# Two transformer blocks on one core: the expert stage's DMAs change queues, its last three blocks stay on chip, and a selection is computed earlier

## The reference, cut to what matters

```python
def moe(x2, w_router, router_bias, w1, w3, w2):
    expert_idx, gate_w = route(x2, w_router, router_bias)      # 2 of 16 experts for each token
    ...
    # the 1024 assignments are sorted by expert and padded to whole blocks
    def run_block(args):
        e, toks = args
        xb = x_pad[toks]
        h = jax.nn.silu(xb @ w1[e]) * (xb @ w3[e])
        return h @ w2[e]
    yb = lax.map(run_block, (blk_e, slot_tok.reshape(n_blk, MOE_BLOCK)))
    y = yb.reshape(-1, D) * slot_gate[:, None]
    return jnp.zeros((N + 1, D), x2.dtype).at[slot_tok].add(y)[:N]
...
        x = layer_norm(DN_ALPHA * x + mix, ln1_g[l], ln1_b[l])
        ffn = moe(x.reshape(B * S, D), w_router, router_bias, w1[l], w3[l], w2[l]).reshape(B, S, D)
        x = layer_norm(DN_ALPHA * x + ffn, ln2_g[l], ln2_b[l])
```

## Time and profile before

| | us |
|---|---|
| median of 3 runs (3739.15 to 3741.57) | 3740.26 |
| profiled execution, its own time | 3743.44 |
| its span in the trace | 3741.4 |
| mean granted TensorE clock over the span | 0.942 |

### The profile page before, as it was taken

How to read it: one execution, slowest core, us unless ns; L and a number is a source line. 1 busy time by engine, 2 the same in 40 slices (tenths; PEclk the granted TensorE clock), 3 DMA queues, 4 the chain that set the end, 5 groups by cost and what they waited for, 6 DMA issues and landing times. The chain is left out here.

```text
span 3741.4 us, 67546 instructions
## 1 busy us (share of the span) xinstructions
PE 3362.5 (90%) x25782; PEld 1878.2 (50%) x25783; DVE 1370.1 (37%) x2629; ACT 906.5 (24%) x1563; POOL 288.8 (8%) x289
## 2 busy tenths in 40 slices
PE   8998999787879989997877699999998788999998
PEld 5445444566754454445666434434444577444443
DVE  1564112545533751113544531011457555410002
ACT  1124111455521161113544410000113422100000
POOL 1000001322130000003322110000000000000000
PEclk9999999799989999997999889999999878999999
DMA  7112222698431103232987222245111000122221
GB/s 262 57 45 80 71 75 112 241 381 348 186 143 68 56 12 124 78 135 113 379 334 315 86 69 72 74 93 149 68 68 55 1 0 1 56 70 76 78 79 67
DMA packets 79881, 446.92 MB, mean 119 GB/s; under 512 B 10416, under 2 KB 22328, under 8 KB 32896
## 3 DMA queue, kind: packets, MB, share of 16 engines
q0 software_dynamic: 37024, 242.40, 16.9%
q1 hardware_dynamic: 39792, 199.77, 15.1%
q10 hardware_dynamic: 2928, 3.07, 0.2%
HBM read 412.05 MB, written 33.16 MB: 119 GB/s over the span
## 5 line engine op out<-in xcount | busy, mean ns | idle before, releaser
L902 PE MATMUL pb<-arena,streamed 128*128 128x512 f32 x1408 | 612.2, 597 | 7.4 <-DVE arena L1858 6.6
L902 PEld LDWEIGHTS pb<-arena,streamed 128*128 128x128 f32 x1408 | 268.6, 191 | 350.3 <-issue 337.7
L801 PE MATMUL pb<-arena,xT 128*32 x3008 | 357.5, 278 | 56.8 <-issue 33.2
L556 PE MATMUL pb<-xT,streamed 128*128 128x512 f32 x832 | 369.5, 603 | 0.0
L801 PE MATMUL pb<-streamed,xT 128*32 128x128 f32 x9024 | 360.1, 278 | 5.5 <-issue 5.5
L801 PEld LDWEIGHTS pb<-arena,xT 128*32 128x32 f32 x3008 | 325.9, 112 | 75.9 <-issue 69.3
L727 PE MATMUL pb<-xT,streamed 128*128 128x512 f32 x768 | 337.1, 597 | 2.5 <-ACT arena L1237 2.5
L801 PEld LDWEIGHTS pb<-streamed,xT 128*32 128x32 f32 x9024 | 329.2, 112 | 4.8 <-issue 4.8
L928 PE MATMUL pb<-arena,streamed 128*128 128x512 f32 x704 | 306.5, 598 | 8.3 <-DMA streamed<-in_w_tail 5.8
L1257 ACT ACTIVATE streamed<-arena 128x3072 f32 x94 | 260.1, 2767 | 57.5 <-issue 48.9
L556 PEld LDWEIGHTS pb<-xT,streamed 128*128 128x128 f32 x832 | 160.1, 194 | 202.8 <-issue 202.7
(11 more groups left out here) (357 smaller groups left out, 3617.7 us busy)
## 6 DMA issues: line engine op xcount, KB each, us to landing
arena<-in_w_moe POOLq DMA_DIRECT2D x192, 1024.0 KB, 10.6
streamed<-in_w_tail SPq DMA_DIRECT2D x87, 1024.0 KB, 4.9
streamed<-in_w_layer SPq DMA_DIRECT2D x78, 1024.0 KB, 4.9
xT<-xs_dram SPq DMA_DIRECT2D x22, 512.0 KB, 11.7
ys_dram<-xT SPq DMA_DIRECT2D x82, 128.0 KB
xs_dram<-lnw POOLq DMA_DIRECT2D x12, 512.0 KB, 17.6
lnw<-in_ln_par POOLq DMA_DIRECT2D x4, 1024.0 KB, 5.9
rel_dram<-arena POOLq DMA_DIRECT2D x1, 4092.0 KB, 88.0
```

The lines of the kernel that those rows point to most:

```text
L556: last = mm(pb[bank][:, 0:cols], unit(w, u, k), rhs[:, k * cols:(k + 1) * cols], start=(k == 0), stop=(k == KC - 1))
L801: last = mm(pb[m][r0:r0 + MOE_BLOCK, 0:FW], rows, w, start=(k == 0), stop=(k == KC - 1))
L902: last = mm(pb[3 * u + s][:], unit(w, u, k), xn[:, k * S:(k + 1) * S], start=(k == 0), stop=(k == KC - 1))
```

## The change

- The expert weights (`load`, `arrived`) move from GpSimd's program to SyncE's, between two halves of the layer weights' `stream`. Row loads and stores (`load_rows`, `store_y`) move from SyncE to GpSimd. The patterns and sizes of all these DMAs stay.
- Blocks 44 to 46 (ON_CHIP = 3) stay in SBUF in `y_last`, 96 rows of 1024. ACT writes each with four copies of 32x256 in place of one of 128x256. 44 blocks are stored, not 46. `last_sel` picks 96 rows. `last_tile` takes 96 rows and 2 matmuls of 512 columns for each tile, where it took 32 rows and 4 of 256. Of the gathers GpSimd now waits for the 44 stores, and for the last block of expert 14, whose weight slot they overwrite.
- DVE computes `sel` before the block tables. PE waits for `route_ready` behind its row selection. ACT runs one tiny Silu right behind the first w1 relay.
- At the end DVE handles one tile after the other: gathered rows, sums, statistics, norm. PE alternates `last_tile` and the transposes.

```diff
@@ constants and buffers
+ON_CHIP = 3
+STORED = N_BLK - ON_CHIP
+OUT_OF = [(STORED + 3 - s) // 4 for s in range(4)]
+LAST = STORED * MOE_BLOCK
...
+        y_last = am[:, 3 * FW:3 * FW + D]
...
@@ sync: what it issues in a layer
-                stream(1, 12)
-
-                def load_rows(j):
...
+                def load(e, p):
+
+                    sp.dma_start(piece(e, p), a["w_moe"][bass.ds((l * N_EXP + e) * PIECES + p, 1)]
+                                 .rearrange("a p n -> p (a n)")).then_inc(expert_loaded[p // 2], 16)
+
+                def arrived(e, m):
+
+                    sp.wait_ge(expert_loaded[m], (l * N_EXP + e + 1) * 32)
                     alone(sp)
-                    sp.dma_start(xs, xs_dram[j * P:(j + 1) * P, :]).then_inc(xs_loaded, 16)
...
+                    sp.sem_inc(expert_here[m], 1)
+
+                stream(1, 6)
+                sp.wait_ge(att_done, l * NT + NT)
+                alone(sp)
+                for p in range(3):
+                    load(0, p)
+                stream(7, 6)
...
+                for e in range(2, N_EXP):
+                    end = sp.value_load(blk_tab[0:1, 2 * N_BLK + e - 2:2 * N_BLK + e - 1], min_val=0, max_val=N_BLK)
+                    for m in range(3):
+                        arrived(e - 1, m)
+                        if m < 2:
+                            sp.wait_ge(up_ready, l * (2 * N_BLK) + 2 * end + 1 + m)
+                        else:
+                            sp.wait_ge(y_ready, l * N_BLK + end + 1)
                         alone(sp)
...
+                        load(e, 2 * m)
+                        load(e, 2 * m + 1)
@@ gpsimd: the same program that sync had, with 44 stores
+                load_rows(1)
                 pool.dma_start(ln_par, a["ln_par"][bass.ds(2 * l + 1, 1), :].rearrange("a n -> (a n)").partition_broadcast(P)).then_inc(ln_loaded, 16)
+                for b in range(STORED):
+                    j = (b + 6) // COLS
+                    if b % COLS == 2 and j < N_TILE:
+                        load_rows(j)
+                    store_y(b)
+
                 pool.wait_ge(route_ready, l + 1)
                 alone(pool)
...
+                end = pool.value_load(blk_tab[0:1, 2 * N_BLK + N_EXP - 2:2 * N_BLK + N_EXP - 1], min_val=0, max_val=N_BLK)
+                pool.wait_ge(y_ready, l * N_BLK + end + 1)
@@ tensor
+                    for n in range(2):
+                        last = mm(last_sums(t, n), last_selT[0:ON_CHIP * MOE_BLOCK, t * P:(t + 1) * P],
+                                  y_last[0:ON_CHIP * MOE_BLOCK, n * S:(n + 1) * S], start=True, stop=True)
                     last.then_inc(last_summed, 1)
@@ scalar
+                    if b >= STORED:
+                        n = (b - STORED) * MOE_BLOCK
+                        for g in range(COLS):
+                            last = fn(y_last[n:n + MOE_BLOCK, g * DW:(g + 1) * DW], pb[2 + b % 2][g * MOE_BLOCK:(g + 1) * MOE_BLOCK, 0:DW], ACT.Copy)
+                        last.then_inc(y_copied, 1)
+                        return
...
                 relay_w1(0, block_expert(act, 0))
+                fn(primed, ones[:, 0:1], ACT.Silu)
                 copy_xsT(0)
@@ vector
                 for t in range(NT):
                     add_gathered(t)
-
-                for t in range(NT):
                     dve.wait_ge(last_summed, l * NT + t + 1)
                     alone(dve)
...
```

More of the change, by code:

```diff
@@ new lines, in arrived @@
+                def arrived(e, m):
+                    sp.wait_ge(expert_loaded[m], (l * N_EXP + e + 1) * 32)
+                    alone(sp)
+                    sp.sem_inc(expert_here[m], 1)
[5 more added lines that the diff above has]
+                stream(7, 6)
+                sp.wait_ge(merged_ready, (l + 1) * 24)
+                alone(sp)
+                for p in range(3, PIECES):
+                    load(0, p)
@@ new lines, in _ @@
+                arrived(0, 0)
+                load(1, 0)
+                load(1, 1)
+                arrived(0, 1)
+                load(1, 2)
+                sp.wait_ge(mix_ready, (l + 1) * 8)
+                alone(sp)
+                load(1, 3)
+                arrived(0, 2)
+                load(1, 4)
+                load(1, 5)
+                sp.wait_ge(route_ready, l + 1)
+                alone(sp)
+                for e in range(2, N_EXP):
[6 more added lines that the diff above has]
+                            sp.wait_ge(y_ready, l * N_BLK + end + 1)
+                        alone(sp)
+                        load(e, 2 * m)
+                        load(e, 2 * m + 1)
@@ L401, in _ @@
+                for m in range(3):
+                    arrived(N_EXP - 1, m)
             for s in range(SLOTS):
@@ L508, in _ @@
-                for m in range(3):
-                    arrived(N_EXP - 1, m)
+                end = pool.value_load(blk_tab[0:1, 2 * N_BLK + N_EXP - 2:2 * N_BLK + N_EXP - 1], min_val=0, max_val=N_BLK)
+                pool.wait_ge(y_ready, l * N_BLK + end + 1)
+                alone(pool)
                 for s in range(4):
-                    pool.wait_ge(y_stored[s], 16 * OUT_OF[s] * (l + 1) + 1)
+                    pool.wait_ge(y_stored[s], 16 * OUT_OF[s] * (l + 1))
                     alone(pool)
@@ L833, in _ @@
                 last.then_inc(xs_tr, 1)
+                pe.wait_ge(route_ready, l + 1)
+                alone(pe)
                 up(0, 0, slot(0), 0)
@@ L1172, in _ @@
                 act.dma_start(dst, src).then_inc(loaded, 16)
-            for s in range(4):
-                act.sem_inc(y_stored[s], 1)
             act.wait_ge(w_loaded[0], 16)
@@ L1710, in _ @@
                 v.tensor_copy(dest[:, :], r_dest).then_inc(dest_ready, 1)
+                n3 = [P, NT, P]
+                for k in range(2):
+                    v.tensor_tensor(cut(sel_b if k else sel, P), pb[7][:, 0:P].unsqueeze(1).to_broadcast(n3),
+                                    r_dest[:, k * NT:(k + 1) * NT].unsqueeze(2).to_broadcast(n3), ALU.is_equal)
+                dve.drain()
+                v.tensor_tensor(sel, sel, sel_b, ALU.add).then_inc(sel_ready, 1)
                 ends = cut(r_cmp[1][:, 0:N_BLK * N_EXP], N_EXP)
@@ L1728, in _ @@
                 v.tensor_copy(blk_tab[:, :], r_tab).then_inc(route_ready, 1)
-                n3 = [P, NT, P]
-                for k in range(2):
-                    v.tensor_tensor(cut(sel_b if k else sel, P), pb[7][:, 0:P].unsqueeze(1).to_broadcast(n3),
-                                    r_dest[:, k * NT:(k + 1) * NT].unsqueeze(2).to_broadcast(n3), ALU.is_equal)
-                dve.drain()
-                v.tensor_tensor(sel, sel, sel_b, ALU.add).then_inc(sel_ready, 1)
                 def relay_w3(b, e):
```

107 lines of the change are left out of this document (30 added, 77 removed).

## The result

The changed kernel takes 3647.51 us (median of 4 runs, 3642.5 to 3650.51), the kernel before 3739.7 in the same comparison: ratio 0.9753, 95% interval 0.9736 to 0.9769. The profiled execution took 3650.51 us.

The account below looks back on a forecast made before the run. TensorE, busy nine tenths of the span, was taken as the bound, with time to win only where it waits, mainly for late rows. 45 + 9.6 + 9.3 - 1 = 63 off 3743.4, median 3.2 lower: 3677 us, range 3650 to 3724.

Parts of the forecast that it names:

- Queues: Expert stages of both layers: stores and rows through GpSimd's queue end the late rows, 45 us gained.
- the lower bound: Expert stages: four store engines have little room, so packing and idle time during waits win only about 30 us.
- upper bound: Expert stages: all that late rows cost TensorE is won, 54.2 us of waits plus 8 at low clock, 62.
- Packing: Stores in GpSimd's queue: 32 packets of 4 KB in place of 128 of 1 KB.
- The spread: Stores in GpSimd's queue: four engines or sixteen, shown by no row; it decides between 30 and 62 us.
- The 3.6 us of a store's 8 turns: Store on four engines beside weights: 8 x (0.29 + 0.16) = 3.6 us, below a block's time, so no backlog.
- Start: Start of the expert stage: earlier selection and table load save 4.8 us a layer, 9.6 in both.
- The table load's 2.6 us: ACT's table load on the way to the second block's relay: moved ahead, it saves 1.28 us each layer.
- End: End of the expert stages: layer 1 ends 9.3 us earlier, layer 0 loses 1.
- A: Rival for GpSimd's queue: stores behave as in the old one, late rows stay, 18 us won, 3722; chance 0.18.
- B: Rival for SyncE's queue: blocked by its own weights, ACT and DVE learn late, 78 us, 3755; chance 0.06.
- C: Rival for the expert stages: TensorE waits for weight relays nearly as long as for rows, 3712; chance 0.08.

Follow-up runs that it names:

- queues_only: The kernel before with only SyncE's and GpSimd's programs changed as in the diff, still 46 stores: 3671.8 us.
- queues_start: queues_only plus the changed start of the expert stage, with the old end and 46 stores: 3660.4 us.
- stores_twice: The changed kernel with each store issued a second time, to a tensor that nobody reads: 3698.3 us.
- rows_on_act: The kernel before with row loads issued by ScalarE on its own queue, stores left on SyncE: 3720.3 us.

## Why the prediction was wrong

The medians of the chain before, `queues_only`, `queues_start`, changed kernel give each part its size: 3737.6, 3671.8, 3660.4, 3647.5. Each of these differences carries the several us said above.

- **Queues: 45 forecast, 66 measured. This is the step that failed.** The mechanism was right: turns of small packets on about four engines, a backlog, rows behind it. What failed was the price: the lower bound and with it "I take 45, the middle of 30 and 62". The lower bound said that four engines with 285 us of packets in 278 us leave little room, and that "weights will do so in part". They did not: waits for relays are 14.4 us in the first stage and 3.8 in the second, and the profile of before, read for the same waits, gives 19.4 and 5.2. Packet times added up to more than the window, which was taken for fullness. In the changed kernel the same sum exceeds its window as well (view of DMAs, 700 to 955 us, first to last load of layer 0):

```profile
DMA packets 18509, 97.07 MB, mean 381 GB/s; under 512 B 5520, under 2 KB 5520, under 8 KB 7824
...
q1 hardware_dynamic: 12009, 87.37, 84.6%
q0 software_dynamic: 6480, 9.50, 10.5%
```

  84.6% of 255 is 216, with 11 for rows and 36 x 8 x 0.16 = 46 for stores 273 us in 255. A sum above the window thus says nothing about a floor. The sixteen engines together are at 95% there (84.6 and 10.5), and still the waits for relays are no more than the 14.4 us above. The loads that the earlier trace rows spread over 278 us went in 255, 381 GB/s in place of 350. The 61.9 us of the stages are the whole upper bound; some 5 of the 66 lie outside the stages, and by its interval the 66 may be 52 to 67.
- **How a store runs.** Packing came out as forecast from the earlier trace rows, 32 packets of 4 KB in place of 128. The spread stayed at about four engines, the case that the forecast gave the low bound, and the full gain came all the same. The 3.6 us of a store's 8 turns, against a block of 6 to 7, was the number to go by, as far as these runs show.
- **Start: 9.6 forecast, 11 and 7 measured** by the two subtractions. From `dest` to the first `up` the stretch is 17.3 us before and 13.8 and 13.3 after. The table load's 2.6 us did not come as worked out: TensorE's wait of 1.96 us at the second block of layer 0 is 1.97 after, now for its own issue, the same wait in layer 1 fell from 3.72 to 1.97, and leaving the early Silu out costs nothing that can be measured.
- **End: 8.3 forecast, 13 measured.** The tile-by-tile reckoning held, 8.1 us earlier for the last norm of layer 1 against 9.3, and about 1 lost in layer 0. What it left out comes behind it: over the stretch from the last `down` to the start of the 37th matmul of the next projection (L902, now L909) 72.2 us became 56.2, and the granted clock of the stretch rose. Before, and then in the changed kernel:

```profile
2113.10:2185.30 72.20, 35.62 (x105) 16.76 (x104) 45.12 (x69) 23.00 (x50) 29.43 (x19) 0.62 0.27 100
```

```profile
2034.90:2091.10 56.20, 34.56 (x87) 16.91 (x88) 37.99 (x61) 24.55 (x53) 24.02 (x12) 0.76 0.21 79
```

  Of these 16 us about 4 are not the end's: `queues_start`, whose end is the old one, has 67.9 us for the same stretch:

```profile
2031.70:2099.60 67.90, 33.65 (x106) 16.84 (x103) 40.14 (x69) 22.94 (x50) 28.90 (x19) 0.59 0.23 80
```

  From there to 56.2 are 11.7 us, 7.4 of them up to the last norm and 4.3 behind it, where the granted clock is higher (0.76 against 0.59 over the stretch). The sum had no term for these 4.3. That the end is worth about 12 us does not hang on one run: from the last `down` of layer 1 to the end of the program the nine profiled kernels with the new end take 1611 to 1622 us, the eight with the old one 1624 to 1632.
- **Rivals.** A (behaves as in the old queue) fell with the row waits: a store still ran on about four engines, but in packets of 4 KB. The Trainium skill's "DMA: Bandwidth & Descriptors", section "Issuing engines are not separate DMA queues", says that starting DMAs on several engines saves only the time of issuing them; that does not hold here, as the same DMAs in other queues are worth 66 us. B (SyncE blocked by its weights) did not come about: no piece took over 1.3 us to issue, and relay waits did not grow. C, weights in the place of rows, did not come about here; `stores_twice` and `rows_on_act` have some of it. A mechanism that no rival named is in `rows_on_act`: with rows free, blocked stores hold up ScalarE, 15.4 and 11.6 us.
- **Sum.** 66 + 11 + 13 = 90 of the 92; the changed kernel's comparison had the kernel before 2 us higher. Against the 63 forecast, 21 us are missing in the queues, 1 in the start and 5 in the end. The 16 to 28 us that a few instructions more or less bring to the changed kernel and its variants are wider than the two small parts, so their sizes rest on the stretches of the traces more than on the totals. Why the kernel before moves by only 6 us is open.

## What to carry to other kernels

Read a store's cut before its bytes: a DMA that runs on few engines, in small packets, beside a stream of large ones can pay a large packet for each small one, and what stands behind it in its queue pays too (here 11.6 us for the issue of a store and 10.8 for the row load behind it). The cure can be on either side, another queue or a cut with more outer runs, and each gave 62 to 66 us here; moving only what waits behind gave 17. Before one per cent is put down to an edit, run the same kernel with an idle instruction more: here two of them moved the total by 28 us.

## What the runs showed of the hardware that was not expected

- The same 128 KB store, 128 runs of 1 KB, keeps about four engines busy as one DMA of 4 x 32 runs and up to 0.5 of the sixteen as four DMAs of 32; its issue took up to 12.4 us in the first form beside the weights, and 1.6 us at most in the second.
- In GpSimd's queue a store of 128 runs became 32 packets of 4 KB and 112 under 512 B, in a burst ahead of them. It took GpSimd 1.4 us to issue (88 in 121.5 us) and GpSimd was idle for 401 us before them.
- TensorE's granted clock over the same 144 us was 0.93 in one and 0.98 in the other of two kernels that differ by two instructions in each layer, the nearest of them 500 us before. Over the whole program it was 0.950 in each of the four runs of the slower variant and 0.954 to 0.956 in the other's.
